# A three-block transformer kernel on one core: block 1's recurrence preparation reordered, and block 3's gate slabs, gates and decays at new places

## The reference, cut to what matters

```python
# block 1: sparse attention, then the RWKV-7 recurrence (r, k, v, low-rank parts w_lo, a_lo, g_lo)
w = -softplus(-(w0 + tanh(w_lo) @ w2)) - 0.5
a = sigmoid(a0 + a_lo @ a2);  g = sigmoid(g_lo) @ g2
kk = k * k_k;  kk = kk / max(sqrt(sum(kk * kk, per head)), 1e-12)
k = k * (1 + (a - 1) * k_a);  decay = exp(-exp(w));  b = kk * a
state = state * d_t + (state @ -kk_t) b_t + v_t k_t;  y_t = state @ r_t
y = (groupnorm(y) * ln_w + ln_b + sum(r * k * r_k) * v) * g
# block 3: mLSTM, GLA and gated delta net (GDN) side by side
qkv = silu(causal_conv(dq, dk, dv));  q, k = l2norm(q) * D**-0.5, l2norm(k)
g_dec = -exp(a_log) * softplus(da + dt_bias);  beta = sigmoid(dbeta)
A = strict_lower(beta * k k^T * decay);  (I + A)^-1 by block doubling
x = x + sum(sigmoid(gates) * (branches @ w_up)) @ w_out
```

## Time and profile before

| what | value |
|---|---|
| time, median of three runs | 3276.92 us (3276.01 to 3278.44) |
| the profiled execution's own time | 3273.09 us |
| its span, first to last instruction | 3271.3 us, mean granted TensorE clock 0.949 |
| busy: TensorE / its weight loads | 2995.1 us (92%) / 2325.2 us (71%) |
| busy: VectorE / ScalarE / GpSimd | 1405.6 / 1155.8 / 1205.4 us |
| 442 low halves on GpSimd | 1096.0 us, 2482 ns each |
| chain that ended last | TensorE 44%, issue 29%, GpSimd 13%, VectorE 8%, ScalarE 4% |

### The profile page before, as it was taken

How to read it: one execution, slowest core, us unless ns; L and a number is a source line. 1 busy time by engine, 2 the same in 40 slices (tenths; PEclk the granted TensorE clock), 3 DMA queues, 4 the chain that set the end, 5 groups by cost and what they waited for, 6 DMA issues and landing times.

```text
span 3271.3 us, 40067 instructions
## 1 busy us (share of the span) xinstructions
PE 2995.1 (92%) x15600; PEld 2325.2 (71%) x15600; DVE 1405.6 (43%) x2024; ACT 1155.8 (35%) x1666; POOL 1205.4 (37%) x559
## 2 busy tenths in 40 slices
PE   7989967979999999889999999979889788999998
PEld 5856636858888886767888887746668466788886
DVE  3007736455221374432273445051376442665442
ACT  4244341344222336334342224233442623542222
POOL 3422512124444452424544443403214122544442
PEclk9998978989999999999999999978899799999999
DMA  3222210032333332225422222302112111622222
GB/s 123 96 77 65 68 30 2 3 130 96 97 97 97 105 128 81 90 74 169 146 95 93 97 97 91 109 23 72 54 49 97 45 40 58 216 97 96 92 96 84
DMA packets 80665, 284.05 MB, mean 87 GB/s; under 512 B 8968, under 2 KB 9096, under 8 KB 79744
## 3 DMA queue, kind: packets, MB, share of 16 engines
q1 hardware_dynamic: 66240, 236.36, 21.8%
q10 hardware_dynamic: 13296, 41.97, 3.4%
q0 software_dynamic: 976, 3.56, 0.4%
HBM read 260.86 MB, written 20.99 MB: 86 GB/s over the span
## 4 chain that ended last, share of the span: by engine, by line
PE 44%; issue 29%; POOL 13%; DVE 8%; ACT 4%; DMA 0%; POOLq 0%; SPq 0%; ACTq 0%; DVEq 0%
POOL slab_r L2716 13%; PE bank L335 11%; PE bank L337 11%; PE bank L336 11%; PE bank L556 2%; PE bank L442 1%; PE bank L533 1%; PE bank L610 1%; PE bank L944 1%; DVE work L2176 1%; DVE small L2174 1%; PE bank L883 1%; PE bank L452 0%; DVE work L2163 0%; PE bank L623 0%
## 5 line engine op out<-in xcount | busy, mean ns | idle before, releaser
L2716 POOL TENSOR_TENSOR slab_r<-slab,slab_high 128x1024 fp32r<-128x1024 f32 x442 | 1096.0, 2482 | 1697.3 <-ACT slab_high L1114 1697.1
L335 PE MATMUL bank<-xh,slab_high 128*128 128x512 f32 x2256 | 902.0, 400 | 30.1 <-POOL slab_r L2716 21.3
L337 PE MATMUL bank<-xh,slab_r 128*128 128x512 f32 x2256 | 884.7, 392 | 0.0
L336 PE MATMUL bank<-x_raw_r,slab_high 128*128 128x512 f32 x2064 | 811.0, 393 | 0.0
L1114 ACT CAST slab_high<-slab 128x1024 fp32r<-128x1024 f32 x442 | 462.3, 1047 | 453.3 <-DMA slab<-in_w_down 215.2
L336 PE MATMUL bank<-work_r,slab_high 128*128 128x512 f32 x1376 | 546.2, 397 | 0.0
L335 PEld LDWEIGHTS bank<-xh,slab_high 128*128 128x128 f32 x2256 | 428.2, 190 | 141.5 <-issue 26.0
L335 PE MATMUL bank<-work_r,slab_high 128*128 128x512 f32 x1184 | 474.7, 401 | 49.0 <-DVE work_r L1916 24.9
L337 PEld LDWEIGHTS bank<-xh,slab_r 128*128 128x128 f32 x2256 | 427.8, 190 | 92.7
L337 PE MATMUL bank<-work_r,slab_r 128*128 128x512 f32 x1184 | 474.7, 401 | 0.0
L336 PEld LDWEIGHTS bank<-x_raw_r,slab_high 128*128 128x128 f32 x2064 | 392.5, 190 | 79.8 <-issue 1.7
(11 more groups left out here) (465 smaller groups left out, 2861.1 us busy)
## 6 DMA issues: line engine op xcount, KB each, us to landing
slab<-in_w_down SPq DMA_DIRECT2D x88, 512.0 KB, 3.2
slab<-in_w_up SPq DMA_DIRECT2D x64, 512.0 KB, 3.2
slab<-in_w_gates SPq DMA_DIRECT2D x56, 512.0 KB, 3.3
slab<-in_w_merge SPq DMA_DIRECT2D x48, 512.0 KB, 3.8
slab<-in_w_gu SPq DMA_DIRECT2D x44, 512.0 KB, 3.5
slab<-in_w_in_a SPq DMA_DIRECT2D x32, 512.0 KB, 3.5
gates<-staging ACTq DMA_DIRECT2D x56, 256.0 KB, 3.0
slab<-in_w_out SPq DMA_DIRECT2D x24, 512.0 KB, 3.2
```

Of the source, the lines that this page charges most:

```text
L335: first = pe.matmul(bank[b][:, :], wh, mh, start=start, stop=False)
L336: pe.matmul(bank[b][:, :], wh, ml, start=False, stop=False)
L337: end = pe.matmul(bank[b][:, :], wl, mh, start=False, stop=stop)
L2716: pool.tensor_tensor(slab_low[:, slot, :], slab[:, slot, :], plain(slab_high[:, slot, :]), ALU.subtract).then_inc(S("slab_split"), 1)
```

## The change

The change moves work and renames tiles; no product is added or removed.

- Attention takes three gate products per step instead of four. Four gate slabs go into the recurrence's preparation: one between the key sums, one behind the second low-rank group, two behind the `r k` sums.
- The low-rank weights are loaded at the start of attention, to tiles 12 to 14. Keys are scaled, squared and summed first; low-rank groups follow one by one, and VectorE takes scans and keys group by group. The decay differences come after the keys. The two 2048-wide multiplications move from GpSimd to VectorE, behind `operands_ready`.
- Block 3: two gate slabs before the mLSTM and two before GLA's levels, four instead of six around the GDN preparation (two of them between the 16 key products), none in the inverse's levels, eight products in each state.
- ScalarE's and VectorE's decay rows move from behind `in_d` to the end of the mLSTM. `in_d` is split in 12 slabs and, after the row broadcasts, 4. ScalarE's last gates of GLA are sent before the last head's norm.
- The values are turned before the key products and the scaled operands after them; the order of VectorE's norms, scales and row differences changes, and some waits between its operations go.

```diff
-EARLY_2, EARLY_M, EARLY_L = 7, 3, 6
+EARLY_2, EARLY_M, EARLY_L = 7, 5, 8
+        AHEAD_M, AHEAD_L, IN_GDN, FIRST_D = 16, 16, (16, 16), 12
-        IN_ATTENTION, IN_SEQUENCE, IN_MLSTM, IN_GLA, IN_LEVEL, IN_STATE = 4, 0, 6, 1, 3, 4
-        AFTER_ATTENTION = 16
-        IN_GDN = (16, 32)
+        IN_ATTENTION, IN_SEQUENCE, IN_MLSTM, IN_GLA, IN_LEVEL, IN_STATE = 3, 0, 6, 1, 0, 8
+        AFTER_ATTENTION = 12
+        KEYS, SQUARES, RK, LOW_RANK = 8, 48, 0, (12, 13, 14)
+        ROW, ROW_WORK = 58, 59
+        VALUES = (60, 61, 16, 17)
 # TensorE, block 1
+            low_rank(0)
+            mark("key_sums")
             for c in range(4):
-                sum_tiles([W(28 + c)], 4 + c % 2, "dve", pair, S("kk_square"))
+                sum_tiles([W(SQUARES + c)], 7, "dve", pair, S("kk_square"))
+                early_gates(2)
+            low_rank(1)
+            early_gates(DC)
+            low_rank(2)
+            low_rank(3)
             for c in range(4):
-                sum_tiles([W(28 + c)], 4 + c, "dve", pair, S("rk_ready"))
+                sum_tiles([W(RK + c)], 4 + c, "dve", pair, S("rk_ready"))
+            early_gates(16 * DC - early[0])
 # TensorE, block 3
+            early_gates(AHEAD_M)
             pe.wait_ge(S("gates_ready"), n.next(S("gates_ready")))
...
             for t in range(NT):
+                if t == 2:
+                    early_gates(AHEAD_L)
                 turn([(W(8 + c)[:, t * P:(t + 1) * P], c * P) for c in range(4)], 6 + t % 2, "act")
...
-            dense("in_d", 16, DC, xnk, ["act"], None)
+            dense("in_d", FIRST_D, DC, xnk, ["act"], None)
             mark("gdn")
             early_gates(IN_GDN[0])
...
-            early_gates(IN_GDN[1])
-            pe.wait_ge(S("operands_ready"), n.next(S("operands_ready")))
+            dense("in_d_rest", 16 - FIRST_D, DC, xnk, ["act"], None)
+            mark("gdn_slabs_done")
+            pe.wait_ge(S("kq_ready"), n.next(S("kq_ready")))
+            pe.wait_ge(S("values_scaled"), n.next(S("values_scaled")))
...
                     pe.matmul(bank[b][:, 0:2 * P], W(22 + h)[:, ch * P:(ch + 1) * P], kq[:, h,
...
+                    early_gates(1)
+            pe.wait_ge(S("operands_ready"), n.next(S("operands_ready")))
+            for t in range(NT):
+                cs = slice(t * P, (t + 1) * P)
+                tokens = turn([(W(34 + c)[:, cs], c * P) for c in range(4)], 4 + t % 2, "act")
 # ScalarE, block 1
+            for c in range(4):
+                act.wait_ge(S("kk_raw"), n.next(S("kk_raw")))
+                act.activation(W(SQUARES + c), W(KEYS + c), ACT.Square).then_inc(S("kk_square"), n.up(S("kk_square")))
...
+            low_rank(0)
+            low_rank(1)
             for c in range(4):
+                act.wait_ge(evac_by["dve"], handed_at["key_sums"]["dve"] + c + 1)
+                act.activation(W(SQUARES + c), W(SQUARES + c), ACT.Ln).then_inc(chain, n.up(chain))
...
+            send_gates(0, 13)
+            low_rank(2)
+            low_rank(3)
+            send_gates(0, 14)
...
+            send_gates(0, 16)
 # ScalarE, block 3 (behind mLSTM: beta, softplus of the decay row, exp(a_log), as before behind in_d)
+            send_gates(0, 32 + AHEAD_M // DC)
...
+            act.activation(W(17)[32:36, :], W(17)[32:36, :], ACT.Sigmoid)\
+                .then_inc(S("beta_ready"), n.up(S("beta_ready")))
...
+            early[1] += AHEAD_L
+            send_gates(0, 32 + EARLY_M + AHEAD_L // DC)
...
+            send_gates(0, 32 + EARLY_M + EARLY_L)
             head_out(3)
             head_square(3)
...
-            send_gates(0, 32 + EARLY_M + EARLY_L)
...
+            copy_tiles("in_d", FIRST_D, W3(0, FIRST_D))
+            act.wait_ge(S("conv3_keys"), n.next(S("conv3_keys")))
+            act.activation(W(18, 8), W(18, 8), ACT.Silu).then_inc(chain, n.up(chain))
 # VectorE, block 1: keys first, then per group c: scans, keys, r k; then the decay differences; then
             dve.wait_ge(S("operands_ready"), n.own(S("operands_ready")))
+            dve.tensor_tensor(W(8, 4), W(52, 4), W(48, 4), ALU.mult).then_inc(chain, n.up(chain))
+            dve.tensor_tensor(W(12, 4), W(20, 4), W(48, 4), ALU.mult)\
+                .then_inc(S("operands_ready_2"), n.up(S("operands_ready_2")))
 # GpSimd
             biases(0)
+            pool.wait_ge(evac_by["act"], handed_at["attention"]["act"])
+            for i, name, rows in zip(LOW_RANK, ("w2a2", "g2a", "g2b"), (P, P, 32)):
+                pool.dma_start(W(i)[0:rows, :], a[name]).then_inc(S("lora_loads"), 16)
...
-            pool.dma_start(W(59), a["w2a2"]).then_inc(S("lora_loads"), 16)
-            pool.dma_start(W(60), a["g2a"]).then_inc(S("lora_loads"), 16)
-            pool.dma_start(W(61)[0:32, :], a["g2b"]).then_inc(S("lora_loads"), 16)
-            pool.tensor_tensor(W(8, 4), W(52, 4), W(48, 4), ALU.mult).then_inc(chain, n.up(chain))
-            pool.tensor_tensor(W(12, 4), W(20, 4), W(48, 4), ALU.mult)\
+            low_parts(16 - AFTER_ATTENTION)
```

More of the change, by code:

```diff
@@ L654, in _, with low_rank @@
             mark("rwkv")
-            pe.wait_ge(S("lora_ready"), n.next(S("lora_ready"), 3))
-            pe.wait_ge(S("lora_loads"), n.next(S("lora_loads"), 48))
-            for c in range(4):
+            def low_rank(c):
                 s = slice(c * P, (c + 1) * P)
+                wa, g0, g1 = (W(i) for i in LOW_RANK)
                 if last[4]:
                     pe.wait_ge(*last[4])
-                pe.matmul(bank[4][:, :], W(59)[0:HD, s], W(28)[0:HD, :], start=True, stop=True)\
+                pe.matmul(bank[4][:, :], wa[0:HD, s], W(28)[0:HD, :], start=True, stop=True)\
                     .then_inc(psum_for["act"], hand(4, "act"))
@@ L1789, in _ @@
                 act.copy(W(18 + t), bank[4 + t % 2][:, :]).then_inc(evac, n.up(evac))
-                act.wait_ge(evac, n.own(evac))
-            for t in range(NT):
-                act.wait_ge(psum_for["act"], n.next(psum_for["act"]))
-                act.copy(W(34 + t), bank[4 + t % 2][:, :]).then_inc(evac, n.up(evac))
                 act.wait_ge(evac, n.own(evac))
@@ L2195, in _ @@
                         .then_inc(S("shift_done"), n.up(S("shift_done")))
-            dve.wait_ge(evac_by["act"], handed_at["rwkv"]["act"] + 12)
             for c in range(4):
+                dve.tensor_scalar(W(KEYS + c), W(20 + c), V("kk", c), None, ALU.mult)\
+                    .then_inc(S("kk_raw"), n.up(S("kk_raw")))
+            dve.tensor_scalar(SM(40, 4), vec[:, VEC["ka"][0]:VEC["ka"][0] + 4], -1.0, 1.0, ALU.mult, ALU.add)\
+                .then_inc(chain, n.up(chain))
+            dve.wait_ge(chain, n.own(chain))
+            for c in range(4):
+                dve.wait_ge(psum_for["dve"], n.next(psum_for["dve"]))
+                dve.tensor_scalar(W(SQUARES + c), bank[7][:, :], 1e-24, 2.0 ** 30, ALU.max, ALU.mult)\
+                    .then_inc(evac, n.up(evac))
+            for c in range(4):
+                dve.wait_ge(evac_by["act"], handed_at["rwkv"]["act"] + 3 * c + 2)
                 for t in range(NT):
@@ L2498, in _ @@
                 dve.wait_ge(sig, n.own(sig))
+            r = slice(32, 36)
+            dve.wait_ge(S("lf_parts"), n.next(S("lf_parts")))
+            dve.scalar_tensor_tensor(W(ROW_WORK)[r, :], W(ROW)[r, :], 0.0, W(ROW_WORK)[r, :], ALU.max, ALU.add)\
+                .then_inc(chain, n.up(chain))
+            dve.wait_ge(chain, n.own(chain))
+            dve.tensor_scalar(W(ROW_WORK)[r, :], W(ROW_WORK)[r, :], SM(60)[r], -1.0, ALU.mult, ALU.mult)\
+                .then_inc(chain, n.up(chain))
+            dve.wait_ge(chain, n.own(chain))
+            for t in range(NT):
+                cs = slice(t * P, (t + 1) * P)
+                sig = S("decay_row") if t == NT - 1 else chain
+                dve.tensor_tensor_scan(W(ROW)[r, cs], ones[r, :], W(ROW_WORK)[r, cs], 0.0, ALU.mult, ALU.add)\
+                    .then_inc(sig, n.up(sig))
+            dve.wait_ge(S("decay_row"), n.own(S("decay_row")))
             dve.wait_ge(S("lf_parts"), n.next(S("lf_parts")))
```

220 lines of the change are left out of this document (97 added, 123 removed).

## The result

| | time, median (range) | profiled execution |
|---|---|---|
| before, four runs | 3276.47 us (3274.95 to 3278.44) | span 3271.3, clock 0.949 |
| after, four runs | 3226.92 us (3224.77 to 3228.85) | span 3222.9, clock 0.955 |

The ratio is 0.9855, with a 95% interval of 0.9838 to 0.9872: faster, and the medians differ by 49.6 us. The forecast was 3227 us.

A forecast was written before the change was run, and what follows sets the result against it. TensorE's own work bounds the kernel, so only holes can shrink: -10 + 2 + 3 + 4.5 + 3.5 - 46 - 24 + 16 = -51, less an allowance of 1: -50, 3227 us against the median. Range 3214 to 3241, 8 in 10 3206 to 3252.

The forecast's parts named there:

- What bounds the kernel: Whole kernel: TensorE's own work fills the long stretches and no product is removed; only holes in the preparations can shrink.
- Attention: Three gate products per step instead of four: -10 us, ends -5.4 (last eight steps only) and -20.
- The allowance for the other 24: Attention's steps where VectorE's top-k loop mostly sets the pace: 4.6 of their 16.3 us are won.
- Preparation: Block 1's recurrence: earlier keys against longer VectorE chain and four low-half collisions; +2 us, ends -6 and +8.
- Decay rows: Moved to the mLSTM's end: in_l's third slab waits behind them for its high half; +4.5 us, ends 0 and +9.
- mLSTM: Block 3: only its entry was given a cost, +3 us for two slabs; the mLSTM itself stood at 0.
- in_d to the mats: Block 3, from in_d into the first inverse level: holes close and two slabs leave; 164 us, -46, ends -54 and -30.
- the third slab's: in_d's third slab waits behind the heads' norm on ScalarE and VectorE's operations: 5 us.
- Levels: Inverse levels without gates: 36 products leave 12 levels, 3.2 us apart at full clock; -24 us, ends -26 and -10.
- States and end: Eight products per state (+11), 24 instead of 20 at the end plus a wait: +16 us, ends +10 and +20.
- this rival: Attention's top-k steps and inverse levels: TensorE's clock falls where filling was taken out; +33 us, 3310, chance 0.03.
- One sign that was to show the forecast wrong: Inverse levels: a clock under 0.9 there would show the forecast wrong.

The follow-up runs named there:

- e3_no_slabs_in_prep: Changed kernel with four gate products per attention step again and no gate slab in the recurrence's preparation, new order kept; 3227.57 us, ratio 0.9852 to the kernel before.
- e4_levels_filled: Changed kernel with three gate products per inverse level again, four per state, four left for the end; 3233.6 us, ratio 0.9873 to the kernel before.
- e10_decays_before_keys: Changed kernel with VectorE's decay differences made ahead of the last two key groups; 3225.3 us, ratio 0.9854 to the kernel before.
- e1_block1: Kernel before with only block 1's part of the change (attention and the recurrence's preparation), block 3 as before; 3264.33 us, ratio 0.9968.
- e12_without_decays_edit: Changed kernel with in_l's bank and high-half edits, two low halves out of preparation, mLSTM gates later, in_d and silu edit; 3205.88 us, ratio 0.9798 to the kernel before.

## Why the prediction was right, point by point

- **What bounds the kernel**: right. The products are all there, and 36 us of holes and 12 of busy time went.
- **Attention**: the last eight steps as said (4.77 us for 4.8). The allowance for the other 24 (4.6 of their 16.3 us) isn't in the profiled pair: -5.9 in all, where the end -5.4 stands for the last steps alone. The other executions say the same, compared like with like: nine that reached the attention late took 161.6 us on average with three products per step, and 167.6 twice with four; the early ones took 163.7 twice, and 171.9 in `e3_no_slabs_in_prep`. That is -6 and -8, so the term of -10 was too large.
- **Preparation**: mechanism right, the sum within the scatter. Keys are there 27.9 us after the attention (32 forecast); all four collisions cost 8.4 (8.2). The removal of two of them gave 4.4 us at once. The whole took 73.3 us in the profiled pair's kernel, but 75.3 on average in the seven kernels that share it, as much as the 75.4 and 75.2 with the old order: 0 for +2, and not surely the pair's -2.1.
- **Decay rows**: right in kind and size, but hidden in the changed kernel behind a wait that the prediction missed, the bank of the 37th gate. Two waits of 4.5 us lay side by side, and one of them was paid. The sum came out (+5.8 for +4.5) for a reason that was only half the stated one.
- **mLSTM**: the step that is missing. The prediction counted the low halves of moved slabs as VectorE's cost in block 1 and not here, though the same two engines meet. Sending the gates later gave back 1.9 of the 5.1 us, with collisions of 2.9 us still there; 4.6 of the 5.1 lie in the first head, which also ran at a lower clock.
- **in_d to the mats**: 163.9 us for 164, but up to the first inverse's start; to the prediction's own end it is some 168, -42 for -46, still inside its ends. Of the waits in it, the third slab's was 5.05 (5 forecast), the one before the values' copies 3.71 (3.5).
- **Levels**: the level itself right (3.15 for 3.18), the gain too small (-28.6 for -24), outside the end of -26 given. It was worked out as 36 products of 0.68; in place each cost 0.79 by this pair, and 0.85 in `e4_levels_filled`.
- **States and end**: +18.6 for +16, a product at 0.78 and not 0.68 in the states.
- **Rivals**: the clock did not collapse where filling was taken out: 0.92 in the attention, and levels 3.15 us apart. The Trainium skill, "TensorE: Matmul & The Clock Gate", section "HAM oscillation — how this bites in real kernels", tells of a kernel whose compute between two waits was shorter than the wait, and which was throttled at each. That is not the case of the levels, so the page didn't speak for this rival as the prediction had it: behind the head of each inverse their waits are under 0.3 us, and the trace shows no repeated throttling there. One sign that was to show the forecast wrong did come, a clock under 0.9 in the levels' stretch (0.89). It was a poor sign: the half clock lies at the heads of the two inverses, behind waits of 2.37 and 3.34 us, where the first level's matmuls take 1.97 us for 1.46.

So misses of 5 us cancelled, levels against mLSTM; that the time came out at 3227 to the microsecond is in part luck. The range of 3214 to 3241 would have held either miss alone.

## What to carry to other kernels

A slab moved into a hole takes its helpers along: ask on which engine its high and low half, its copy and its bank fall at the new place, since a low half on GpSimd cost VectorE's chain 2.1 us each time in the preparation, and a changed count of gates put the last one into the bank that the next stage starts with. When a wait is explained, look for the one behind it: in in_l removing the first alone gave nothing, removing both gave 5.7 us. A small operation put ahead of table loads or a norm on the queue of the helping engine can be worth more than a move of slabs: one `high_next` took in_l from 93.7 to 88.3 us, two of them and a later silu took 11.4 us out of in_d's stretch.

## What the runs showed of the hardware

The stretch ahead of the attention, the same code in all kernels, took 257.5, 257.9 and 258.7 us in three of the fourteen profiled executions, and 264.8 to 267.7 in the others. Block 3's stretches agree within 0.2 us between most executions (the mLSTM of `e10_decays_before_keys`, 98.0 us for 99.2 with the same code, is an exception). The granted clock tells the two kinds apart: from 200 to 255 us it was 0.91 in the three, and 0.75 to 0.81 in the eleven. Up to 240 us the two shown here are alike; from 245 to 260 the changed kernel runs at 0.50 and `e1_block1` at 1.00. First the changed kernel, then `e1_block1`:

```profile
200.00:255.00 55.00, 42.24 (x109) 20.03 (x108) 14.19 (x26) 31.76 (x58) 2.40 (x1) 0.80 0.14 48
```

```profile
200.00:255.00 55.00, 41.49 (x120) 18.99 (x118) 16.90 (x31) 34.27 (x62) 2.40 (x1) 0.91 0.14 48
```

Why the clock falls at another time in the same code stays open. Part of the 7 to 9 us is given back by the masked products, since the early executions took longer for attention and preparation. Only one execution of a kernel is profiled, so that this makes a kernel's shorter runs isn't shown. It would fit `e3_no_slabs_in_prep` and `e12_without_decays_edit`, where the profiled execution, an early one, is one of two that took 5 to 7 us less than the other three. In any case a single trace of block 1 can't resolve a few us.
